# A quarter of the gate logits computed inside attention, two PSUM banks for the rest, and out-of-range places in the experts' gathers and scatters

## The reference

```
h = rmsnorm(x);  p = h @ w_in              # columns: MLA latents | RWKV-7 inputs | gate logits (2*1024)
o_a = multi-head latent attention (8 heads, chunk-causal, query tiles of 128 rows)
o_b = RWKV-7 time mixing (delta-rule state, chunks of 128 rows here)
x = x + sum_n sigmoid(gate_logits_n) * (o_n @ w_out[n])
h2 = rmsnorm(x)
x = x + experts(h2)     # 32 experts, each row to 2 of them: (silu(h2 @ w_gate[e]) * (h2 @ w_up[e])) @ w_down[e]
```

## Time and profile before

| | us |
|---|---|
| median of 3 runs | 1756.04 (1746.57 to 1762.42) |
| profiled execution, its own time | 1758.26 |
| its span in the profile | 1756.4 |
| TensorE busy in it | 1532.3 (87%) |
| VectorE busy | 868.0 (49%) |
| ScalarE busy | 445.4 (25%) |

### The profile page before, as it was taken

One profiled execution on the slowest core, in us unless ns is written; L12 is line 12 of the kernel. 1 busy time (PEld: TensorE's weight loads), 2 busy tenths in 40 slices (PEclk: granted clock), 3 DMA queues, 4 the chain that ended last, 5 costly groups with the idle time before them and its releaser, 6 DMA issues. The chain is left out here.

```text
span 1756.4 us, 38861 instructions
## 1 busy us (share of the span) xinstructions
PE 1532.3 (87%) x16348; PEld 1077.3 (61%) x16348; DVE 868.0 (49%) x1878; ACT 445.4 (25%) x873; POOL 104.4 (6%) x131
## 2 busy tenths in 40 slices
PE   4999999959999999999994888879993988888893
PEld 3888888825666656666673566545552756666662
DVE  2445455454657666765764666636673122111110
ACT  2222222232223313322311333334542111111010
POOL 0000000000000000000000000000001112332320
PEclk9999999979999999999996999989995989999997
DMA  9322233442222132211123544249522999999972
GB/s 327 143 88 85 84 99 99 174 156 94 83 92 82 64 99 82 73 64 61 61 61 91 184 95 95 68 135 363 202 104 93 352 340 333 333 338 339 324 210 32
DMA packets 102430, 272.35 MB, mean 155 GB/s; under 512 B 32400, under 2 KB 51472, under 8 KB 92800
## 3 DMA queue, kind: packets, MB, share of 16 engines
q1 hardware_dynamic: 94528, 244.85, 41.2%
q0 software_dynamic: 7744, 25.19, 6.3%
HBM read 206.06 MB, written 64.77 MB: 154 GB/s over the span
## 5 line engine op out<-in xcount | busy, mean ns | idle before, releaser
L526 PEld LDWEIGHTS a_ps<-a_hT,a_wz 128*128 128x128 f32 x1792 | 202.6, 192 | 3.8 <-issue 3.8
L526 PE MATMUL a_ps<-a_hT,a_wz 128*128 128x128 f32 x1792 | 204.0, 275 | 0.0
L1823 PE MATMUL d_ps<-wo,d_oT 128*128 128x512 f32 x288 | 130.6, 603 | 0.8 <-DVE d_oT L1643 0.8
L1992 DVE COPY f_xT<-f_turned 128x384 f32<-128x384 f32 x32 | 17.8, 557 | 193.9 <-PE f_turned L1959 193.9
L1823 PEld LDWEIGHTS d_ps<-wo,d_oT 128*128 128x128 f32 x288 | 53.4, 192 | 59.4 <-issue 57.9
L1985 PE MATMUL f_down<-wd,f_midT 128*96 128x512 f32 x160 | 82.2, 663 | 1.8 <-DVE f_midT L2004 1.8
L2183 DVE TENSOR_SCALAR f_y<-f_down,table 96x512 f32<-96x512 f32 x32 | 23.9, 747 | 112.7 <-PE f_down L1985 112.7
L1096 PE MATMUL b_ps<-r_wg,r_hT 128*128 128x512 f32 x128 | 65.5, 645 | 16.2 <-POOL b_S L756 12.8
L1437 ACT ACTIVATE c_probs<-c_score,c_top 128x1024 f32<-128x1024 f32 (+8 forms) x72 | 50.5, 702 | 102.5 <-DVEq L1415 96.5
L816 DVE TENSOR_TENSOR b_M<-b_ps,r_causal 128x512 f32<-128x512 f32 x72 | 46.4, 686 | 59.6 <-PE b_ps L1155 59.1
L2190 ACT ACTIVATE f_xT<-f_turned 128x384 f32<-128x384 f32 x32 | 15.7, 490 | 232.1 <-PE f_turned L1959 232.1
(11 more groups left out here) (353 smaller groups left out, 2896.7 us busy)
## 6 DMA issues: line engine op xcount, KB each, us to landing
wgu<-w_gate_up SPq DMA_DIRECT2D x20, 2048.0 KB, 18.2
f_wgu<-w_gate_up SPq DMA_DIRECT2D x12, 2048.0 KB, 18.6
wd<-w_down SPq DMA_DIRECT2D x20, 1024.0 KB, 11.9
f_wd<-w_down SPq DMA_DIRECT2D x12, 1024.0 KB, 11.1
r_hT<-hT_d SPq DMA_DIRECT2D x18, 512.0 KB, 4.0
b_hT<-hT_d SPq DMA_DIRECT2D x18, 512.0 KB, 4.1
gate_d<-b_logits SPq DMA_DIRECT2D x32, 256.0 KB, 2.7
zm_d<-a_zm SPq DMA_DIRECT2D x9, 896.0 KB, 4.7
```

The source lines that it names most:

```text
L526: mm = pe.matmul(banks[Z_BANKS[n % 2]][:, j * P:(j + 1) * P], wz[:, i, (g + j) * P:(g + j + 1) * P], hT[t % 2][:, i, :], start=(i == 0), s ...
L1823: mm = pe.matmul(banks[2 + u][:], oT[t % 2][:, HB * branch(u) + k, :], wo[:, HB * branch(u) + k, half(u)], start=(k == 0), stop=(k == HB - 1))
```

## The change

**Mixing.** `UNITS` goes from 4 to 3, so 27 items instead of 36, and `FILL_OF` from 28 matmuls a stage to 20. Items alternate between two PSUM banks (`FILLS`), so an item waits for the copy of the item before the last one. The second bank is won by letting `NORMS` (key norms and bonus factors) share the bank `XD`, with four added waits. The three weight units have a buffer each, and the fourth is loaded into the first one's when unit 0 is done.

**Attention.** The fourth unit is computed here: `gate_part` puts one matmul of 128x512 into each of the first 8 of a head's 9 steps, between the scores and the product with the values, so a head does one tile; `last_gates` does the sample tile after the last head. ScalarE copies `fill` at each head's last step, and SyncE stores it and loads the rows `hT` two tiles ahead. The 8 stores of zeros (4 MB) fall away.

**Experts.** Empty places and table entries without a cell now carry an index out of range, and every indirect DMA has `bounds_check` with `oob_is_err=False`. The four `xg` buffers are set to zero once by GpSimd, `h2_d` and `out` lose their spare tiles, and the table its trash columns.

```
-    UNITS, UW = 4, 512
+    UNITS, UW = 3, 512
-        NORMS, XD, WY, C0, C1, FILL = range(2, 8)
+        XD, WY, C0, C1 = range(2, 6)
+        FILLS = (6, 7)
-        FILL_OF = (2, 2, 3, 2, 3, 2, 3, 4, 2, 1, 2, 2)
+        FILL_OF = (1, 1, 2, 2, 2, 2, 2, 3, 1, 1, 1, 2)
 # fill (TensorE)
-                        after(pe, logits_copied, q)
+                        after(pe, logits_copied, q - 1)
-    mm = pe.matmul(banks[FILL][:], hT[q % 2][:, k, :], wg[u % 2][:, k, :], ...)
+    mm = pe.matmul(banks[FILLS[q % 2]][:], hT[q % 2][:, k, :], wg[u][:, k, :], ...)
 # waits of TensorE for the shared bank XD: in lora, values, right_side, state
+                after(pe, x_copied, n - 1)
+                pe.wait_ge(nn_ready, n + 1)
+                pe.wait_ge(bon_copied, min(t + 2, NT))
+                pe.wait_ge(nn_ready, min(t + 3, NT))
 # attention, TensorE, step p of head j
                     if p + 2 < ROUND + ahead:
                         scores(u, p + 2)
+                    gate_part(u, j, p % STEPS)
                     pe.wait_ge(turn_dve, G + 1 + START)
+            def gate_part(u, j, k):
+                if k == DC:
+                    return
+                if k == 0:
+                    pe.wait_ge(hT_in[j], 16 * u + 16 + START)
+                    pe.wait_ge(fill_copied, u * 2 + j + START)
+                mm = pe.matmul(fill[:], hT[j][:, k, :], wg[:, k, :], start=(k == 0), stop=(k == DC - 1))
+                if k == DC - 1:
+                    mm.then_inc(fill_done, 1)
 # attention, ScalarE, at a head's last step
+                    if p % STEPS == STEPS - 1:
+                        act.wait_ge(fill_done, u * 2 + j + 1 + START)
+                        act.wait_ge(logits_stored[1 - j], 16 * (u + j) + START)
+                        act.activation(logits[:], fill[:], ACT.Copy).then_inc(fill_copied, 1)
 # attention, SyncE, after a head's rows are stored and the next but one is loaded
+                    sp.wait_ge(fill_copied, u * 2 + j + 1 + START)
+                    sp.dma_start(io["gate_d"][...][:, UNIT:, :], logits[:]).then_inc(logits_stored[j], 16)
+                    if ahead:
+                        load_hT(u * 2 + 2 + j, j)
-            for g in range(NG):
-                sp.dma_start(io["h2_d"][NT + g], nothing[:]).then_inc(no_rows_set, 16)
-                sp.dma_start(io["out"][NT + g], nothing[:]).then_inc(no_rows_set, 16)
 # experts, GpSimd, each indirect DMA
-                 bass.IndirectOffsetOnAxis(ap=index[...][:, 0:1], axis=0)).then_inc(s["x_in" + str(b)], 16)
+                 bass.IndirectOffsetOnAxis(ap=index[...][:, 0:1], axis=0),
+                 bounds_check=NT * P - 1, oob_is_err=False).then_inc(s["x_in" + str(b)], 16)
 # experts, GpSimd, once each for xg[2] and xg[3]; xg[0] and xg[1] at the start of merge
+                pool.memset(xg[e][:], 0.0).then_inc(s["index_set"], 1)
-OUTPUTS = dict(out=(NT + NG, P, D), ...
+OUTPUTS = dict(out=(NT, P, D), ...
```

More of the change, by code:

```diff
@@ L718, in _ @@
             load_wg(1)
+            load_wg(2)
             q = 0
@@ L1113, in lora @@
                 after(pe, bon_copied, n)
+                after(pe, x_copied, n - 1)
                 for p in range(PAIRS):
[L1115 removed]
+                    mm = pe.matmul(banks[XD][:, p * P:(p + 1) * P], same_head[:], kn[:, p, :], start=True, stop=True)
                 mm.then_inc(lora_done, 1)
@@ L1302, in attention @@
         acc = ps("acc", [P, 512])
+        fill = ps("fill", [P, 512])
+        UNIT, UW = 3, 512
+        QUADS = [slice(DEC * n, DEC * n + DEC) for n in range(P // DEC)]
+        FOLDED = UW // len(QUADS)
+        hT = [sb(f"hT{j}", [P, DC, P]) for j in range(2)]
+        logits = sb("logits", [P, UW])
+        wg = early["wg"][0]
         ident = sb("ident", [P, P])
@@ L1318, in attention @@
         out_stored = [sem("out_stored0"), sem("out_stored1")]
-        nothing, begun = sb("nothing", [P, D]), keep["begun"]
+        fill_done, fill_copied = sem("fill_done"), sem("fill_copied")
+        hT_in, logits_stored = ([sem(f"{n}{j}") for j in range(2)] for n in ("hT_in", "logits_stored"))
+        begun = keep["begun"]
         prime(nc, [s for s in sems if not s.name.endswith("_step")] + list(keep["weights_in"].values()))
@@ L1375, in _ @@
             rounds(sp, body)
-            sp.wait_ge(no_rows_set, 32 * NG + START)
+            sp.wait_ge(fill_copied, NT + START)
+            for n, rows in enumerate(QUADS):
+                sp.dma_start(io["gate_d"][NPT, 0:DEC, UNIT, n * FOLDED:(n + 1) * FOLDED], logits[rows, 0:FOLDED]).then_inc(logits_stored[0], 16)
             for j in range(2):
                 sp.wait_ge(out_stored[j], 16 * ROUNDS + START)
-        @block.gpsimd
-        def _(pool):
-            pool.memset(nothing[:], 0.0).then_inc(nothing_set, 1)
+                sp.wait_ge(logits_stored[j], 16 * (ROUNDS + len(QUADS) * (1 - j)) + START)
         @block.vector
@@ L1451, in body @@
                         act.activation(probsT[:, 4:n, :], turned[1][:, 0:(n - 4) * P], ACT.Copy).then_inc(turn_act, 1)
+                    if p % STEPS == STEPS - 1:
+                        j = head_of(p)
+                        act.wait_ge(fill_done, u * 2 + j + 1 + START)
+                        act.wait_ge(logits_stored[1 - j], 16 * (u + j) + START)
+                        act.activation(logits[:], fill[:], ACT.Copy).then_inc(fill_copied, 1)
+                if not ahead:
+                    act.wait_ge(fill_done, NT + START)
+                    act.wait_ge(logits_stored[1], 16 * ROUNDS + START)
+                    act.activation(logits[:, 0:FOLDED], fill[:, 0:FOLDED], ACT.Copy).then_inc(fill_copied, 1)
             exponential(0, 0)
@@ L1499, in body, with last_gates @@
                     mm.then_inc(pv_done, 1)
+            def gate_part(u, j, k):
+                if k == DC:
+                    return
+                if k == 0:
[4 more added lines that the diff above has]
+                    mm.then_inc(fill_done, 1)
+            def last_gates():
+                pe.wait_ge(hT_in[0], 16 * (ROUNDS + 1) + START)
+                pe.wait_ge(fill_copied, NPT + START)
+                for k in range(DC):
+                    for n, rows in enumerate(QUADS):
+                        mm = pe.matmul(fill[rows, 0:FOLDED], hT[0][:, k, 0:DEC], wg[:, k, n * FOLDED:(n + 1) * FOLDED],
+                                       start=(k == 0), stop=(k == DC - 1), tile_position=(0, DEC * n))
+                mm.then_inc(fill_done, 1)
+            pe.wait_ge(early["wg_last_in"], 16)
             scores(0, 0)
@@ L1623, in _ @@
             pool.memset(table[:], 0.0)
+            for e in range(EARLY):
+                pool.memset(xg[e][:], 0.0)
             pool.memset(run[:], 0.0).then_inc(set_done, 1)
@@ L2077, in scatter @@
                 pool.indirect_dma_start(io["table_d"], bass.IndirectOffsetOnAxis(ap=cell[t][k][:, 0:1], axis=0),
-                                        entry[:, t, k, :], None).then_inc(scattered, 16)
+                                        entry[:, t, k, :], None,
+                                        bounds_check=P * BLOCKS - 1, oob_is_err=False).then_inc(scattered, 16)
             def work(n):
@@ L2252, in layer @@
                 ("causal", [2 * P]), ("first", [2, P]), ("merge_mask", [5, P // 4]), ("state_given", [PAIRS, P]))},
-            **{n: c.enter_context(nc.semaphore("r_" + n)) for n in ("consts_in", "zm_in0", "hT_in0", "wg_in0", "head_in0")},
+            **{n: c.enter_context(nc.semaphore("r_" + n)) for n in ("consts_in", "zm_in0", "hT_in0", "wg_in0", "head_in0", "wg_last_in")},
         )
```

80 lines of the change are left out of this document (48 added, 32 removed).

## The result

The changed kernel takes 1737.2 us (median of 4 runs, 1735.9 to 1737.9), the kernel before beside it 1758.1: a ratio of 0.9885, 95% interval 0.9861 to 0.991. It is faster by 1.15%, 20 us. A later comparison gave 0.9903 (0.9866 to 0.994). The forecast was 1736.

What follows compares the result with a forecast made beforehand. TensorE was taken to set the pace in mixing and attention, with the DMA engines full in the experts. 1758.3 - 62 (mixing) + 46 (attention) - 4 (experts) = 1738, the median 2.2 lower: 1736 us, range 1706 to 1757.

Steps and rivals of the forecast that it cites:

- Bank waits, 15.9 us: Mixing: TensorE's waits for ScalarE to empty the one bank of the fill items leave, 15.9 us.
- New waits, 1.4 us a stage: Mixing: with fill matmuls gone, TensorE waits longer at slot 11 (0.86) and next stage's start (0.52): 11 us over 8 stages.
- Mixing, 62 us less: Mixing: removed matmuls, folded item and bank waits give 72.9 us, new waits take 11; bounds 50 and 66.
- Attention, 46 us more: Attention: 64 added matmuls cost 61 us, 18 fill idle time, the end adds 3; bounds 37 and 60.
- The end of attention, 3 us: End of attention: folded item, its copy and four stores come after the last value product, 3 us; bounds 2 and 6.
- Pair, 16 us gained: Mixing and attention together: 62 less and 46 more, 16 us gained; stated bounds about -5 and 28.
- the fourth rival: Attention: gate matmuls find no gap; 1766 us at the bounds, about 1754 half way; chance 0.10.
- Experts, 4 us: Experts: the first eight DMA engines still move all their rows, so skipping empty places only eases contention, 4 us.
- The first rival: Experts: empty places spread over all engines, another 23 us gained, 1713 us; chance 0.28.
- That skipped rows cost as much as moved ones: Experts: out-of-range rows become transfers of the same cost, leaving 16 us gained, 1740 us; chance 0.12.
- A slower GpSimd instruction: Experts: index checks lengthen GpSimd's gather and scatter; over twice as long each, 35 us lost, 1775 us; chance 0.07.
- Memsets ahead of the first gathers, nothing: Start of experts: two memsets delay the first gathers by about 1.48 us at most, costed at nothing.

Runs made afterwards that it cites:

- x5: The kernel before with two banks for logits in mixing and XD shared by the norms, all four gate units still in mixing: 1740.4 us.
- x4: The changed kernel with its 20 fill matmuls placed differently, one more in slots 0 and 10, one less in 8 and 9: 1717.6 us.
- x12: The changed kernel with its 20 fill matmuls placed oppositely, one less in slots 0 and 10, one more in 8 and 9: 1772.7 us.
- x8: The changed kernel with the folded item at the end of attention copied into a tile of its own: 1736.6 us beside 1737.5.
- x1: The kernel before with the change of mixing and attention alone, the experts as before: 1744.3 us.
- x2: The kernel before with the experts' part alone (new merge, experts and tables, no zero rows stored): 1750.2 us.
- x3: The changed kernel with an expert's 96 places renumbered, partition c standing for place c % 6 * 16 + c // 6: 1717.2 us.
- x6: The changed kernel with an expert's 96 places renumbered, partition c standing for place c % 16 * 6 + c // 16: 1735.0 us.

## Why the prediction was right, point by point

The total, 1738 worked out for the profiled execution and 1737.9 measured (its span is 1736.0), came out right by terms that erred in both directions: mixing gave 15 us less than forecast, attention cost 10 less and the experts gave 6 more in the traces. That these cancel so closely is luck. The mechanisms came out as forecast but for the clock in mixing and the end of the program, both below.

**Bank waits, 15.9 us: right.** x5 shows them alone, 16 us.

**Price of a matmul in mixing, 0.86: right.** From x5 to x4, neither of which waits long, the stage lost 58.53 - 51.47 = 7.06 us for 8 matmuls, 0.88 each.

**New waits, 1.4 us a stage: right in place and size.** 0.36 + 0.86 was worked out before the merge of slot 11 and 1.21 measured, 0.52 at the next stage's start and 0.5 measured. The predicted stage, 60.57 - 6.88 - 1.99 + 1.38 = 53.08, is the 53.09 above.

**Mixing, 62 us less: 46.7, below the bound of 50.** This is the term that failed, and by its own criterion that part of the prediction did. (The bound was also added up wrongly: its own conditions give 72.9 - 27.5 - 5.3 = 40.) The step that failed was to multiply one undisturbed stage by 8 and to leave out what waits do to the clock. From one bonus product to the one eight stages later the kernel before took 481.2 us (8 x 60.57 = 484.6) and the changed one 427.8 (8 x 53.09 = 424.7). Against the eight equal stages that loses 3.4 us before, where the first stage is 54.66 and not 60.57, and 3.1 after, where the clock costs some 8 (three stages of 54.67, 56.20 and 56.67) and two shorter first stages (49.13 and 51.78) give 5 back. The stretch ahead of the eight is 1.9 longer, with a clock of 0.57 between 396 and 400 us. The last 56.50 us, 51.78 before, have a clock of 0.79 instead of 0.90: 4.7 us more. The 2.0 us of the folded item had been taken off outside the eight stages too, where the time grew instead. Together 15.1 of the missing 15.3. That low clock follows new waits is shown by x4 and x12; that the last stretch has the same reason is not, since x4 has it as well.

**Attention, 46 us more: 35.9, below the bound of 37.** (That bound keeps the price of 0.95; at 0.86 a matmul, the lower price that the prediction names, it is 64 x 0.86 - 24 + 2 = 33.) The filled idle time was sized about right, 16 us (24.1 to 8.2) for the 18 taken, with the wait for `c_probsT` down by 14.1. The price was too high. TensorE's busy time grew by 49.6 us, 47.6 without the folded item, 0.74 a matmul for the 0.95 taken. One reason is again the clock, now in favour: the head shown in the earlier trace rows had 0.92, and one after has 1.00, in 27.30 us instead of the forecast 29.7:

```profile
1057.00:1084.30 27.30, 26.65 (x236) 16.21 (x235) 15.66 (x46) 9.37 (x23) 0.00 (x0) 1.00 0.43 105
```

**The end of attention, 3 us: 4.2.** A whole chain and the item were the upper bound; the wait of 6.30 us for the one tile was overlooked. The trace of x8 gives back 2.

**Pair, 16 us gained: 10.8** in the traces; x1 says 12.6 (0.9928 of 1756). Both large terms were overestimated, and most of the error cancels. (Two more of its numbers are off: the stated ends give the pair -10 to 29, not -5 to 28, and the fourth rival half way 1751, not 1754.)

**Experts, 4 us: 7.5 by x2, 10.4 in the first pair of traces.** The mechanism agrees with x3 and x6: six neighbouring places an engine, full engines that set the end, and the contention of the others eased. Only its size was low. The first rival, an even spread, was not the state of the changed kernel, but it names what was there to be had: 27 us for the stage, and 1355.3 to the end was 401.1 us before and 373.3 in x3, 27.8 less.

**Rivals.** That skipped rows cost as much as moved ones is out: 20.4% of the engines for 27.9. That they are dropped is not quite right either: they go as packets of 4 and 8 bytes. A slower GpSimd instruction is out too: by the means of the stage the scatter takes 1.46 us in both kernels and the gather 1.00 for 0.95. The gate matmuls did find gaps in attention.

**Memsets ahead of the first gathers, nothing: right.** The first expert's matmuls to the third's took 27.3 us for 25.9, but not for the memsets: it is 27.1 in x1, which has none there, and 26.2 in x2, which has them, and TensorE waits in none of these traces for the third or fourth expert's rows.

**The end of the program: overlooked, 3 us lost.** From TensorE's last matmul to the end it is 27.5 us for 24.7, and so in the other traces with the experts' part (x2 27.5, x4 27.5, x6 27.7, against 24.6 in x1 and x5). Up to the last packet of the last scatter nearly all is the same (1738.1 of 1756.4 before, 1714.9 of 1736.0 after). Behind it GpSimd goes through its loop for rows over 96 (`overflow`), 22 turns of which none has work here. By its branches in the trace this takes 9.66 us before and in x1 and x5, and 12.85 in the changed kernel and every trace with the experts' part: 0.44 and 0.58 us a turn. So the bounds checks in the skipped body come with 3.2 us more on GpSimd. About 0.4 of it was hidden before, where TensorE's own way through the loop ended at 1756.15 us, behind GpSimd's last step at 1755.73. Why a turn takes longer was not tried. Without it the experts' part would be worth 7.5 + 2.8, some 10 us (an estimate).

## What to carry to other kernels

Filler work is cover: when some of it leaves, list after which instruction each engine is late, and spend what remains there first; here one table of twelve numbers with the same sum was worth from 15 us gained to 35 lost, more than the move. Sum the change part by part on the chip too: two spare banks gave 16 of the 20 us, and the move that gave the change its name cost 4 to 9 us until the cover was placed right. When part of a DMA is skipped, ask which engine loses rows: bytes saved on engines that were not last bring little, and a renumbering made 7.5 us into some 25. Look at the end of the program as well: 22 empty turns of a loop stand there for 10 to 13 us.

## What was not expected of the hardware

A short wait of TensorE can cost more than its length. With waits of 1.9 and 1.6 us at the turn of a stage instead of 1.2 and 0.5 the granted clock over 380 us of mixing fell from 0.98 to 0.93, and the kernel lost 35 us, about half of it not idle time but slower matmuls; without them it was 1.00. The kernel before, with more idle time than the changed one, stayed at 1.00.

An indirect DMA whose index is out of range still issues a packet for the row, of 4 or 8 bytes, and the queue took 20.4% of the engines' time for 27.9 with 69% of the rows. Where the empty rows stand makes 18 us more or less, as if each engine had six neighbouring rows of 96 (x3 and x6).

A loop of GpSimd whose body is skipped still costs 0.44 us a turn here, and 0.58 with bounds-checked DMAs in the body.
